# One product of 512 columns in four output projections

## The chip, the core and the metric

The kernel runs on one core of a Trainium2 chip. The metric is the device time of one launch in microseconds (us). Lower is better. All weights stay in HBM and are streamed in once per launch; the residual stream `x` (256 tokens, 2048 features) stays in SBUF from the first to the last layer.

## What is computed

Two model blocks run one after the other on one sequence of 256 tokens. All that matters here is where the output projections stand in them; everything is in float32.

```python
def first_block(x, ...):
    for l in range(2):
        h = rms_norm(x, norm_g[l])
        ...                                   # three kinds of attention on h
        x = x + y @ w_out[l]                  # 2048 x 2048: a changed projection
    return rms_norm(x, final_g)

def second_block(x, ...):
    for layer in range(2):
        x = layer_norm(ALPHA * x + mixers[layer](x), *ln1[layer])      # not changed
        x = layer_norm(ALPHA * x + conv_ffn(x, *ffns[layer]), *ln2[layer])

def conv_ffn(x, w_gate, w_val, conv_w, conv_b, w_down):
    h = causal_dwconv(x @ w_gate, conv_w) + conv_b
    return (jax.nn.silu(h) * (x @ w_val)) @ w_down      # 5632 x 2048: a changed projection
```

## The kernel before

Activations lie feature by token: a tile is 128 features (partitions) by 256 tokens (columns), so `x` is 16 tiles. A weight matrix is cut into output tiles of 128 features, and each of these into blocks of 128 by 128, one for each 128 input features. 1024 columns of such blocks (8 blocks, 512 KB) are one load, numbered `n` in the order of the whole program; the last load of a `down` tile has 4 blocks.

To keep float32 precision with the one-pass type fp32r, each operand is held in two parts: a high part (the value rounded to fp32r) and a low part (the rest). A block's product is three matmuls of 256 columns that add up in one PSUM region: high weight by high `x`, high weight by low `x`, low weight by high `x` (`col`, lines 1948 to 1950). Each matmul loads its own 128 x 128 weights, so the high weight block is loaded twice in a row. Such a set of three matmuls is called a block below.

A load passes through four engines. SyncE fetches it to one of `NRAW` = 4 raw buffers (`fetch`, line 3356, waits until the low part of load n - 4 is made). ScalarE makes the high part (`hi`, line 2380; there are `NPAIR` = 4 buffers for pairs, so it waits until TensorE has used load n - 4). VectorE subtracts to make the low part (`lo`, line 2691). TensorE waits for the low part and runs the blocks (`col`), and its last matmul of the load counts `used`.

Every engine runs its own instructions strictly in the order of one plan, written while the kernel is built. `load(n)` (line 482) puts `hi(n + 2)` and `lo(n + 1)` into the plan ahead of the matmuls of load n. `pump()` after each load lets every side generator take one step; among these is `Norm.step` (line 672), which for each pair of `x` tiles centres the tiles (in the layer norms), sums them, squares them on ScalarE (line 2405) and adds the squares, and makes the raw parts for the next stage.

`out_proj` (line 878) is the output projection of four places: `w_out` of both layers of the first block and `down` of both FFNs. Where its argument `first` is given (`w_out`), tiles 0 to 3 run through `four`, which the change leaves alone; tiles 4 to 15 run in the loop at the end. For `down` all 16 tiles run in the loop. The loop takes two output tiles at a time: they share one PSUM bank of 512 columns, 256 each (`col_tile`, line 534), and when both are done VectorE adds the whole bank to two tiles of `x` in one instruction (`x_add`, line 2816, its instruction is profile line 2819), after which the bank is free and the norm's step for the pair is queued. A `w_out` tile has 16 blocks in two loads, a `down` tile 44 blocks in six loads. The mixers of the second block have a projection of their own (`out_half`), which keeps `col_tile`.

Of the kernel before, what the change touches and what calls it, by code (L numbers as in the profile page):

```python
# [320 lines left out]
def v3(ap, n):  # L321
    return ap.rearrange("p (a b) -> p a b", a=n)


def _build(nc, a, out, stages, ctx):
# [172 lines left out]
    side = []  # L498
# [35 lines left out]
    def col_tile(o, keys, rhs, ready, bk, step=8):  # L534
# [10 lines left out]
        return (used, n)  # L545

    def col_group(outs, tiles_, rhs, ready, after, norm=None, done=None):
        for half in range(2):
            for (o, opens), key in zip(outs, tiles_):
                n = load(*key, half)  # L550
                do("col", n, o, rhs, 8 * half, half == 0 and opens, half == 1,
                   [ready_at(ready, 8 * half + q) for q in range(8)], after)
                pump()
                if half and done is not None:
                    done.append((used, n))
            if norm:
                norm.read[half] = (used, n)
        return (used, n)
# [319 lines left out]
    def out_proj(parts, y, ready, alpha, norm, first, xt):  # L878
# [12 lines left out]
        for t in range(4 if first else 0, KT, 2):  # L891
            bk = banks.get()
            p2 = v3(bk.view, 2)
            for j in range(2):
                m = col_tile(p2[:, j, :], parts(t + j), y, ready, bk)
            add(bk, t, m)
        if norm.free is None:
# [1037 lines left out]
    def tensor_program(e):  # L1935
# [4 lines left out]
        def col(n, o, rhs, k0, begin, end, ready, after, part=None):  # L1940
# [10 lines left out]
            if q == c - 1:  # L1951
                last.then_inc(*used(n))

        def row(n, ps, lhs, k0, ready, after):
            (wh, wl), (lh, ll) = pair_of(n), lhs
# [387 lines left out]
        def ret_pv(j, hh):  # L2343
# [6 lines left out]

        steps = dict(norm_cols=norm_cols, col=col, row=row, rms_sq=rms_sq, ln_first=ln_first, norm_sums=norm_sums, scores=scores,
                     p_turn=p_turn, pv=pv, rope_mm=rope_mm, ukv_k=ukv_k, ukv_v=ukv_v, uq=uq, head_sum=head_sum,
# [329 lines left out]
    def vector_program(e):  # L2682
# [133 lines left out]
        def x_add(sid, bk, t, alpha, m, xt):  # L2816
# [3 lines left out]
                                   op1=ADD).then_inc(*vec("x_add", sid, t))  # L2820

        def q_scale(j):
            w.on([j.q_m])
# [444 lines left out]
        def ret_decay(j, hh):  # L3268
# [5 lines left out]
            else:  # L3274
# [5 lines left out]
                     norm_acc=norm_acc, norm_var=norm_var, norm_R=norm_R, norm_ln=norm_ln, norm_rms=norm_rms, norm_cols=norm_cols, gains=gains, raw_lo=raw_lo,  # L3280
                     lead_fix=lead_fix, lead_scale=lead_scale, x_add=x_add,
                     q_scale=q_scale, k_scale=k_scale, k_copy=k_copy, gate_evict=gate_evict, rope_mm=rope_mm, rope_fin=rope_fin,
# [266 lines left out]
```

## Time and profile before

| what | value |
|---|---|
| time, median of 3 runs | 3592.99 us (3585.59 to 3611.3) |
| span of the profiled execution, first to last instruction | 3590.3 us |
| TensorE matmul busy | 95% of the span, 30164 matmuls |
| VectorE busy | 64% |
| ScalarE busy | 45% |
| mean granted TensorE clock | 0.975 |
| HBM read | 581.31 MB, 162 GB/s over the span |

The profile is of one execution. Its page shares out the span by engine and by line; views of the trace show single instructions with their start and duration. The duration shown for a matmul is the time through the array (some 280 ns for one of 256 columns) and overlaps that of the next, so a matmul's price is read from the distance between two starts, or from the number of matmuls in a stretch. The weight loads have rows of their own (engine PEld).

### The profile page before, as it was taken

The numbers are of one execution on the slowest core, as the hardware profiler recorded it, in microseconds if no ns is written. First come the engines' busy times: TensorE is split into PE (matmuls) and PEld (weight loads), VectorE is DVE, ScalarE is ACT, GpSimd is POOL, SyncE is SP. The second block draws the span as 40 slices with busy tenths as digits, with TensorE's granted clock in tenths as the row PEclk, the third lists the DMA queues.
The fourth block names the chain that finished last, engine by engine and source line by source line (L and its number), as shares of the span: only waits on it lengthen the run. The fifth ranks groups of instructions, "written<-read, shape, count | busy, mean of one in ns | idle before, by whom it ended". The sixth has DMA issues, their size and how long they took to land.

```text
span 3590.3 us, 68886 instructions
## 1 busy us (share of the span) xinstructions
PE 3425.7 (95%) x30164; PEld 3358.8 (94%) x30164; DVE 2281.9 (64%) x3711; ACT 1603.8 (45%) x2267; POOL 81.6 (2%) x101
## 2 busy tenths in 40 slices
PE   7899999999998998999999999988998999999997
PEld 7899999999998888899999999987998999999997
DVE  5656556556676678697666655687545976666555
ACT  4544445444445523255444444562433554444443
POOL 0000000000000001000000000002000000000000
PEclk9999999999999989999999999999999999999998
DMA  6455555555454322255555666541443556656664
GB/s 227 146 176 172 169 176 177 174 179 171 159 194 134 106 66 69 82 171 182 194 189 197 196 191 192 188 131 64 166 158 112 169 174 198 195 189 197 193 195 132
DMA packets 162637, 587.88 MB, mean 164 GB/s; under 512 B 18144, under 2 KB 18144, under 8 KB 161952
## 3 DMA queue, kind: packets, MB, share of 16 engines
q1 hardware_dynamic: 160848, 575.06, 49.0%
q0 software_dynamic: 1488, 8.42, 0.7%
q8 instruction: 236, 3.87, 0.4%
q14 instruction: 65, 0.53, 0.1%
HBM read 581.31 MB, written 2.10 MB: 162 GB/s over the span
## 4 chain that ended last, share of the span: by engine, by line
PE 51%; DVE 9%; ACT 1%; issue 1%; POOL 0%; ACTq 0%; DVEq 0%; POOLq 0%
PE bank L1948 15%; PE bank L1950 15%; PE bank L1949 15%; DVE pairs L2691 2%; DVE xs L2807 1%; DVE xs L2805 1%; PE bank L2127 0%; PE bank L1963 0%; PE bank L1964 0%; PE bank L1965 0%; DVE xr L2695 0%; PE bank L2114 0%; DVE xr L2775 0%; DVE right L3133 0%; PE bank L2104 0%
## 5 line engine op out<-in xcount | busy, mean ns | idle before, releaser
L1948 PE MATMUL bank<-xr,pairs 128*128 128x256 f32 (+1 forms) x5920 | 1675.2, 283 | 62.1 <-DVE pairs L2691 50.7
L1949 PE MATMUL bank<-xr,pairs 128*128 128x256 f32 (+1 forms) x5920 | 1650.9, 279 | 0.0
L1950 PE MATMUL bank<-xr,pairs 128*128 128x256 f32 (+1 forms) x5920 | 1650.5, 279 | 0.0
L2380 ACT ACTIVATE pairs<-raw 128x1024 fp32r<-128x1024 f32 x1108 | 1144.4, 1043 | 980.7 <-PE bank L1950 867.0
L2691 DVE TENSOR_TENSOR pairs<-raw,pairs 128x1024 fp32r<-128x1024 f32 x1108 | 1312.8, 1203 | 324.3 <-ACT pairs L2380 321.9
L1948 PEld LDWEIGHTS bank<-xr,pairs 128*128 128x128 f32 x5920 | 1124.0, 190 | 75.9 <-DVE pairs L2691 58.8
L1949 PEld LDWEIGHTS bank<-xr,pairs 128*128 128x128 f32 x5920 | 1123.0, 190 | 1.6
L1950 PEld LDWEIGHTS bank<-xr,pairs 128*128 128x128 f32 x5920 | 1123.5, 190 | 0.0
L1948 PE MATMUL bank<-parts,pairs 128*128 128x256 f32 x1792 | 497.4, 278 | 3.6 <-DVE parts L2695 3.3
L1949 PE MATMUL bank<-parts,pairs 128*128 128x256 f32 x1792 | 495.6, 277 | 0.0
L1950 PE MATMUL bank<-parts,pairs 128*128 128x256 f32 x1792 | 495.6, 277 | 0.0
L1948 PEld LDWEIGHTS bank<-parts,pairs 128*128 128x128 f32 x1792 | 337.3, 188 | 4.5 <-DVE pairs L2691 3.8
L1949 PEld LDWEIGHTS bank<-parts,pairs 128*128 128x128 f32 x1792 | 337.2, 188 | 0.2
L1950 PEld LDWEIGHTS bank<-parts,pairs 128*128 128x128 f32 x1792 | 337.2, 188 | 0.0
L3107 DVE TENSOR_SCALAR arena<-bank,vec 128x256 f32<-128x256 f32 x88 | 47.8, 543 | 229.9 <-PE bank L1950 229.9
L2819 DVE SCALAR_TENSOR_TENSOR xs<-xs,bank 128x512 f32<-128x512 f32 x64 | 43.7, 686 | 174.6 <-PE bank L1950 174.5
L1963 PE MATMUL bank<-pairs,xr 128*128 128x256 f32 x512 | 149.1, 291 | 0.0
L1965 PE MATMUL bank<-pairs,xr 128*128 128x256 f32 x512 | 143.4, 280 | 0.0
L1964 PE MATMUL bank<-pairs,xr 128*128 128x256 f32 x512 | 143.3, 280 | 0.0
L1963 PEld LDWEIGHTS bank<-pairs,xr 128*128 128x128 f32 x512 | 97.0, 189 | 0.8
L1964 PEld LDWEIGHTS bank<-pairs,xr 128*128 128x128 f32 x512 | 96.9, 189 | 0.7
L1965 PEld LDWEIGHTS bank<-pairs,xr 128*128 128x128 f32 x512 | 96.7, 189 | 0.0
(589 smaller groups left out, 3122.4 us busy)
## 6 DMA issues: line engine op xcount, KB each, us to landing
raw<-in_w_in SPq DMA_DIRECT2D x176, 512.0 KB, 4.3
raw<-in_gate SPq DMA_DIRECT2D x176, 512.0 KB, 4.7
raw<-in_val SPq DMA_DIRECT2D x176, 512.0 KB, 4.0
raw<-in_down SPq DMA_DIRECT2D x160, 512.0 KB, 4.5
raw<-in_l_w_in SPq DMA_DIRECT2D x146, 512.0 KB, 3.9
raw<-in_w_out SPq DMA_DIRECT2D x64, 512.0 KB, 4.6
raw<-in_l_w_out SPq DMA_DIRECT2D x64, 512.0 KB, 3.7
raw<-in_v_in SPq DMA_DIRECT2D x48, 512.0 KB, 4.7
```

Source lines behind the costliest of these rows:

```text
L1948: mm(o, wh[:, q, :], rh[:, k, :], start=begin and q == 0, stop=False)
L1949: mm(o, wh[:, q, :], rl[:, k, :], start=False, stop=False)
L1950: last = mm(o, wl[:, q, :], rh[:, k, :], start=False, stop=end and q == c - 1)
L1963: mm(o, lh[:, k, ms], wh[:, q, :], start=k == 0 and m == 0, stop=False)
L1964: mm(o, ll[:, k, ms], wh[:, q, :], start=False, stop=False)
L1965: last = mm(o, lh[:, k, ms], wl[:, q, :], start=False, stop=k == KT - 1)
L2380: e.activation(pair_of(n)[0], v3(raw_of(n), widths[n] // slices[n]), ACT.Copy).then_inc(*hi_made(n))
L2691: e.tensor_tensor(lo_, v3(raw_of(n), widths[n] // slices[n]), hi_.bitcast(F32), SUB).then_inc(*lo_made(n))
L2805: e.tensor_tensor(xp, xp, two(N.a2), MUL).then_inc(*vec("scaled", N.id, t))
L2807: e.tensor_tensor(xp, xp, two(N.a1), ADD).then_inc(*vec("minus", N.id, t))
L2819: e.scalar_tensor_tensor(out=x[:, t:t + 2, :], in0=x[:, t:t + 2, :], scalar=alpha, in1=v3(bk.view, 2), op0=MUL, op1=ADD).then_inc(*vec("x_ ...
L3107: e.tensor_scalar(b, p2[:, 0, :], VC(f"cw2_{l}", t), VC(f"cb_{l}", t), MUL, ADD).then_inc(*vec("conv2", j.id))
```

## The change

In the loop of `out_proj` each output tile gets a PSUM bank of its own. The high weight block is loaded once and meets a moving operand of 512 columns, made of the high part and the low part of `x` as two runs of 256: the left half of the bank collects high by high, the right half high by low. The low weight block then meets the high part of `x` as before and adds to the left half. VectorE adds both halves to `x` in two instructions per tile, the second waiting for the first. The rest (order of loads, the pumps, the norm's step after each second tile) keeps its place. `parts(t + j)` and the loads are the same.

```diff
+    def wide_tile(bk, keys, rhs, ready):
+
+        k = 0
+        for key in keys:
+            n = load(*key)
+            c = widths[n] // 128
+            do("wide", n, bk, rhs, k, key is keys[0], key is keys[-1], [ready_at(ready, k + q) for q in range(c)])
+            pump()
+            k += c
+        return (used, n)
...
         for t in range(4 if first else 0, KT, 2):
-            bk = banks.get()
-            p2 = v3(bk.view, 2)
             for j in range(2):
-                m = col_tile(p2[:, j, :], parts(t + j), y, ready, bk)
-            add(bk, t, m)
+                bk = banks.get()
+                m = wide_tile(bk, parts(t + j), y, ready)
+                do("x_add_wide", sid, bk, t + j, alpha, m, xt[t] if xt else [])
+                banks.put(bk, (vec, "x_add", sid, t + j))
+            side.append(norm.step(t, (vec, "x_add", sid, t + 1)))
...
+        def wide(n, bk, rhs, k0, begin, end, ready):
+            (wh, wl), (rh, rl), c = pair_of(n), rhs, widths[n] // 128
+            o = v3(bk.view, 2)
+            w.wait_ge(*lo_made[n])
+            if begin:
+                w.on(bk.after)
+            for q in range(c):
+                k = k0 + q
+                w.on(ready[q])
+                a, b = rh[:, k, :], rl[:, k, :]
+                hl = bass.AP(a.tensor, a.offset, [a.ap[0], (b.offset - a.offset, 2), a.ap[-1]])
+                mm(o, wh[:, q, :], hl, start=begin and q == 0, stop=False)
+                last = mm(o[:, 0, :], wl[:, q, :], a, start=False, stop=end and q == c - 1)
+            last.then_inc(*used(n))
...
+        def x_add_wide(sid, bk, t, alpha, m, xt):
+            p2 = v3(bk.view, 2)
+            w.on([m])
+            w.on(xt)
+            e.scalar_tensor_tensor(out=x[:, t, :], in0=x[:, t, :], scalar=alpha, in1=p2[:, 0, :], op0=MUL,
+                                   op1=ADD).then_inc(*vec("x_add_hi", sid, t))
+            w.wait_ge(*vec["x_add_hi", sid, t])
+            e.tensor_tensor(x[:, t, :], x[:, t, :], p2[:, 1, :], ADD).then_inc(*vec("x_add", sid, t))
```

## Rows read from the trace of the kernel before

**Rows 1.** The page: span, then busy us (share) and instructions of each engine.

```profile
span 3590.3 us, 68886 instructions
...
PE 3425.7 (95%) x30164; PEld 3358.8 (94%) x30164; DVE 2281.9 (64%) x3711; ACT 1603.8 (45%) x2267; POOL 81.6 (2%) x101
```

**Rows 2.** The page: the chain that ended last, share of span by line.

```profile
PE bank L1948 15%; PE bank L1950 15%; PE bank L1949 15%; DVE pairs L2691 2%; DVE xs L2807 1%; DVE xs L2805 1%; PE bank L2127 0%; PE bank L1963 0%; PE bank L1964 0%; PE bank L1965 0%; DVE xr L2695 0%; PE bank L2114 0%; DVE xr L2775 0%; DVE right L3133 0%; PE bank L2104 0%
```

**Rows 3.** Four changed stretches: length; busy PE, PEld, DVE, ACT, POOL; clock; DMA share; GB/s.

```profile
482.30:538.80 56.50, 56.50 (x482) 56.50 (x482) 29.91 (x36) 22.77 (x24) 0.00 (x0) 1.00 0.57 187
974.60:1029.00 54.40, 54.40 (x482) 54.40 (x482) 33.92 (x45) 26.24 (x34) 0.00 (x0) 1.00 0.62 200
2126.20:2305.80 179.60, 179.60 (x1587) 179.60 (x1586) 101.27 (x120) 77.52 (x89) 0.00 (x0) 1.00 0.63 194
3386.10:3565.60 179.50, 179.50 (x1585) 179.36 (x1583) 95.28 (x107) 71.28 (x75) 0.00 (x0) 1.00 0.58 179
```

**Rows 4.** Timeline of VectorE, adds of two tiles each: start us, duration us.

```profile
493.51 0.69 DVE L2819 SCALAR_TENSOR_TENSOR xs<-xs,bank 128x512 f32<-128x512 f32 x1 [5.28 <-PE bank L1950]
504.82 0.69 DVE L2819 SCALAR_TENSOR_TENSOR xs<-xs,bank 128x512 f32<-128x512 f32 x1 [5.28 <-PE bank L1950]
...
985.49 0.69 DVE L2819 SCALAR_TENSOR_TENSOR xs<-xs,bank 128x512 f32<-128x512 f32 x1 [4.06 <-PE bank L1950]
...
996.37 0.69 DVE L2819 SCALAR_TENSOR_TENSOR xs<-xs,bank 128x512 f32<-128x512 f32 x1 [4.06 <-PE bank L1950]
...
2186.26 0.69 DVE L2819 SCALAR_TENSOR_TENSOR xs<-xs,bank 128x512 f32<-128x512 f32 x1 [4.42 <-PE bank L1950]
2216.18 0.69 DVE L2819 SCALAR_TENSOR_TENSOR xs<-xs,bank 128x512 f32<-128x512 f32 x1 [4.42 <-PE bank L1950]
```

**Rows 5.** Timeline of TensorE and its weight loads inside a `down` tile.

```profile
2200.00 0.28 PE L1948 MATMUL bank<-parts,pairs 128*128 128x256 f32 x1
2200.01 0.19 PEld L1949 LDWEIGHTS bank<-parts,pairs 128*128 128x128 f32 x1
2200.12 0.28 PE L1949 MATMUL bank<-parts,pairs 128*128 128x256 f32 x1
2200.12 0.19 PEld L1950 LDWEIGHTS bank<-parts,pairs 128*128 128x128 f32 x1
```

**Rows 6.** Timeline of TensorE: plain float32 matmuls with 256 and with 2 columns.

```profile
110.76 1.89 PE L2009 MATMUL bank<-arena 128*128 128x256 f32 x8
...
1505.96 3.63 PE L2092 MATMUL bank<-con,arena 128*128 128x2 f32 x32
```

**Rows 7.** Groups of VectorE instructions by shape: count, busy us, mean ns, idle before.

```profile
L2691 DVE TENSOR_TENSOR pairs<-raw,pairs 128x1024 fp32r<-128x1024 f32 x1068 | 1286.7, 1222 | 306.1 <-ACT pairs L2380 303.7
...
L2819 DVE SCALAR_TENSOR_TENSOR xs<-xs,bank 128x512 f32<-128x512 f32 x64 | 43.7, 686 | 174.6 <-PE bank L1950 174.5
...
L3117 DVE TENSOR_TENSOR arena<-arena,bank 128x256 f32<-128x256 f32 x88 | 36.4, 413 | 0.0
...
L2826 DVE SCALAR_TENSOR_TENSOR arena<-bank,arena 128x256 f32<-128x256 f32 x32 | 13.6, 424 | 98.3 <-PE bank L1950 98.3
...
L3249 DVE SCALAR_TENSOR_TENSOR hs<-hs,vec,bank 128x256 f32<-128x256 f32 x8 | 3.8, 475 | 2.9 <-PE bank L2104 2.9
```

**Rows 8.** Timeline of VectorE just after the add at 2216.18.

```profile
2216.79 2.35 DVE L2691 TENSOR_TENSOR pairs<-raw,pairs 128x1024 fp32r<-128x1024 f32 x2
...
2219.78 0.42 DVE L2726 TENSOR_TENSOR nbuf<-nbuf,xs 128x256 f32<-128x256 f32 x1
2220.24 0.42 DVE L2728 TENSOR_TENSOR nbuf<-nbuf,xs 128x256 f32<-128x256 f32 x1
```

**Rows 9.** The chain that ended last, where the last projection ends.

```profile
3565.54 0.13 PE bank L1950
3565.69 0.70 DVE xs L2819
```

**Rows 10.** DMA issues of `down` weights: count, KB each, median us from issue to landing.

```profile
raw<-in_down SPq DMA_DIRECT2D x160, 512.0 KB, 4.5
```

More of the change, by code:

```diff
@@ L2349, in ret_pv @@
             mm(ps[:, 128:T], s["v"][:, 1, hh, :], s["A"][:, T:T + 128], start=False, stop=True).then_inc(*pe("ret_pv", j.pr, hh))
-        steps = dict(norm_cols=norm_cols, col=col, row=row, rms_sq=rms_sq, ln_first=ln_first, norm_sums=norm_sums, scores=scores,
+        steps = dict(norm_cols=norm_cols, col=col, wide=wide, row=row, rms_sq=rms_sq, ln_first=ln_first, norm_sums=norm_sums, scores=scores,
                      p_turn=p_turn, pv=pv, rope_mm=rope_mm, ukv_k=ukv_k, ukv_v=ukv_v, uq=uq, head_sum=head_sum,
@@ L3280, in vector_program @@
                      norm_acc=norm_acc, norm_var=norm_var, norm_R=norm_R, norm_ln=norm_ln, norm_rms=norm_rms, norm_cols=norm_cols, gains=gains, raw_lo=raw_lo,
-                     lead_fix=lead_fix, lead_scale=lead_scale, x_add=x_add,
+                     lead_fix=lead_fix, lead_scale=lead_scale, x_add=x_add, x_add_wide=x_add_wide,
                      q_scale=q_scale, k_scale=k_scale, k_copy=k_copy, gate_evict=gate_evict, rope_mm=rope_mm, rope_fin=rope_fin,
```

## The prediction

> **What bounds the kernel now.** I read the page's shares first: TensorE is busy for 95% of a span of 3590.3 us, VectorE for 64%, ScalarE for 45% [rows 1]. The chain that ended last says the same by line: 45% of the span is the three matmuls of `col`, and the next line, VectorE's low parts, has 2% [rows 2]. Shares of the whole say little about one stage, so I read the stretches of the four changed projections. In each of them TensorE is busy all the time at a granted clock of 1.00 (its 2.4 GHz level), with VectorE at 53 to 62% and the DMA engines at 57 to 63% [rows 3]. So in these stages time is the number of blocks times the price of a block, and nothing else.
>
> That price comes from the distance between two adds, since each add waits for the end of a pair of tiles. In `down` a pair has 2 x 44 = 88 blocks and takes 2216.18 - 2186.26 = 29.92 us, which is 340.0 ns a block or 113.3 ns a matmul. In `w_out` of layer 1 a pair has 32 blocks and takes 10.88 us: 340.0 ns too. In `w_out` of layer 0 it takes 11.31 us: 353.3 ns a block, 117.8 ns a matmul [rows 4]. The same instructions at the same clock have two paces here. 1585 to 1587 matmuls in 179.5 us confirm the first (113.2 ns), 482 in 56.5 us the second (117.2 ns) [rows 3].
>
> **What sets 113.3 ns.** 256 columns at 2.4 GHz are 106.7 ns, so a matmul costs 6.6 ns more than its columns. Inside a `down` tile every weight load starts within 0.01 us after a matmul has started, and the next matmul starts 0.11 us later [rows 5]. The matmuls with only 2 columns show what is left when there is almost nothing to stream: 32 of them take 3.63 us; less the last one's own 0.25 us that is some 109 ns from start to start [rows 6]. So loading weights takes about 109 ns, and matmuls of 256 columns are paced by it, just above their columns. The opposite case is the plain float32 matmul of line 2009: 8 records take 1.89 us; less the last one's 0.38 us that is 1.51 / 7 = 215.7 ns each [rows 6]. This is 512 / 2.4 = 213.3 plus 2.4 ns; I take it for 512 steps of the array, during which the weight load is hidden and only a small fixed cost remains.
>
> **The change, part by part.** (1) The wide matmul. It replaces two matmuls and one weight load. The nearest row is line 2009's 215.7 ns against 2 x 113.3 = 226.7 ns now. From below it is bounded by its columns, 213.3 ns; from above I use the slower pace of `w_out`, 2 x 117.8 = 235.6 ns. I take 215.7, because it is the row in which the array has the same 512 steps and a weight load runs beneath it.
>
> (2) The low weight's matmul keeps its 256 columns and, beneath it, the load of the next high weight, so it keeps its 113.3 ns (bounds: 109 and 117.8). A block is then 215.7 + 113.3 = 329.0 ns instead of 340.0: 11.0 ns less. Over the two `down` projections this is 2 x 16 x 44 = 1408 blocks x 11.0 = 15.5 us. Over `w_out` of layer 1, 12 x 16 = 192 blocks, 2.1 us. In `w_out` of layer 0 I let the narrow matmul keep its slow pace: 353.3 - 215.7 - 117.8 = 19.8 ns x 192 = 3.8 us. If the slow pace ended there, it would be 24.3 x 192 = 4.7 us. Sum: -21.4 us.
>
> The Trainium skill gives the same two prices, and I cite it as it also holds a rule that would give another result: "TensorE: Matmul & The Clock Gate", section "Back-to-back issue gap", has N / 2.4 + 2.5 ns for warm matmuls, 216 ns for 512 columns, where line 2009 shows 215.7. For the streams of load and matmul of real kernels the same section gives about 131 ns at 512 columns. By that figure the four stages would lose some 171 us; this is the rival "far more" below.
>
> (3) VectorE's adds. A pair had one of 686 ns. A tile now has two of 256 columns. The first is like line 2826's (424 ns) or, if the scalar costs what it does with a vector operand, line 3249's (475 ns); the second like line 3117's, 413 ns [rows 7]. Dependent instructions of this size start 0.46 us apart at 0.42 us each [rows 8], so a tile's add takes 0.46 + 0.41 = 0.87 us (0.92 with 475 ns), 1.74 us a pair, 1.05 us more than now. For 28 pairs (6 + 6 + 8 + 8) that is 29 us more work on VectorE. It is covered where TensorE never waits for it: in a `down` pair VectorE is busy 56% of 29.9 us, so 13 us are idle and 1.05 is asked for [rows 3, 4].
>
> (4) The order on VectorE. Now it stands at an add once per tile, not once per pair, until TensorE has ended the tile. Queued behind it is the low part two loads ahead of the one just ended; the next load's is made already. After the end at T the add starts 0.04 us later (the last matmul's slot ends at 3565.54 + 0.11, the add starts at 3565.69 [rows 9]), takes 0.87 us, and the low part 1.15 to 1.22 us (2.35 for two [rows 8], mean 1222 ns [rows 7]): ready at T + 2.13. TensorE needs it when it has run the load between, 8 x 0.329 = 2.63 us. So 0.5 us of cover is left (it is 0.8 us now), and I cost this at nothing. If the cover went, each 0.1 us over it would cost 56 tiles x 0.1 = 5.6 us. What is late next behind a late low part is SyncE's fetch of the load four on: it leaves at T + 2.1, lands 4.5 us later [rows 10], and its high and low part take some 2.3 us more, T + 8.9 in all; TensorE comes to it five loads after T, at 13.2 us.
>
> In `w_out` a tile lasts only 16 x 0.329 = 5.26 us. The stretch of layer 1 is the tightest: 33.9 us of VectorE in 5 pairs [rows 3], 6.8 a pair, with the wide adds 7.8 of 10.5 us. It still fits.
>
> (5) Ends. At the end of each projection the last add lies open on the chain: now 0.70 us for the pair [rows 9], after the change 0.87 for the last tile (the other tile's is done before). 4 x 0.17 = +0.7 us.
>
> (6) PSUM banks, 14 or 16 taken in turn instead of half as many: 8 exist, a bank comes back after eight tiles when its add is long done. The count of loads, bytes and pumps does not change. Both are costed at zero.
>
> **Sum.** -15.5 - 2.1 - 3.8 + 0.7 = -20.7 us. Made against the profiled execution this is 3590.3 - 20.7 = 3569.6 us of span. The median of the runs shown lies 2.7 us above that span, so I predict 3593.0 - 20.7 = 3572.3 us, 0.6% less.
>
> **The rivals.**
>
> *The cost sticks to each instruction.* The 6.6 ns over the columns belong to every matmul with its load, whatever its length. Then the wide matmul is 213.3 + 6.6 = 220 ns, a block 333.3, and the gain 6.7 x 1600 + (353.3 - 220 - 117.8 = 15.5) x 192 - 0.7 = 13 us: 3580 us. For it: no fp32r matmul in the trace is longer than its weight load. Against it: line 2009. Chance 0.15.
>
> *The two streams disturb each other (the other side).* The two paces of [rows 4] show that something beyond count and clock slows matmuls by 4.5 ns in this kernel. The wide matmul reads two runs of `x` far apart, with the low weight's load beneath the first; now each of the three matmuls meets its weight load in a pattern that lasts for the whole stage. If all blocks went to 353.3 ns, 1600 x 13.3 + 0.7 = 22 us are lost: 3615 us. It decides from a wide matmul above 226.7 ns. Against it: the weight load has twice the time beneath a wide matmul. To be over 1% slower the wide matmul would have to cost 226.7 + 36 / 1792 x 1000 = 247 ns. Chance 0.12, 0.05 of it beyond that. The Trainium skill speaks against this rival: by the same page, section "Step-by-step: what each phase is for", streaming and weight loading have read ports of their own, so that loading takes nothing from the running matmul; by that rule alone the sum above stands, but it doesn't account for the two paces in [rows 4].
>
> *VectorE becomes late.* The gain is used up when each tile loses 20.7 / 56 = 0.37 us, that is when add and low part take 0.87 us more than I count; 1% slower needs 1.0 us a tile. Chance 0.05, 0.03 of it beyond 1%: 3593 to 3630 us.
>
> *It does not do what it says.* The wide product is cut into two of 256 columns with a weight load each, and only the adds differ: 3594 us. Chance 0.04.
>
> *Far more.* The columns alone are 768 / 2.4 = 320 ns a block, 20 x 1600 + 33.3 x 192 = 38 us: 3555 us. By the price of 131 ns (above) it would be 3422 us. Against both: 256 columns take 113.3 ns, more than one step of the clock each. Chance 0.04.
>
> **How the numbers follow.** The forecast has 0.60, the rivals 0.15, 0.12, 0.05, 0.04 and 0.04. The forecast's own range is 3565 to 3582 us. The range of 8 in 10 reaches down to the columns' bound (3556) and up past the case of no gain with the spread of the three runs, to 3602; it leaves out the rest of the disturbed case and of the late VectorE. About 1% (36 us) is what a measurement of this kernel can tell from no change. Faster by more than that is only the last rival, 0.04; slower by more is 0.05 + 0.03 = 0.08; within 1% is 0.88.
>
> **What would show it.** After the change the page should have 1792 matmuls and as many weight loads fewer (28372). In the wide line's stretches a wide matmul should be followed 0.216 us later by the narrow one and that 0.113 us later by the next wide one; two adds of `down` tiles should stand 44 x 0.329 = 14.48 us apart. A distance of 14.67 would be the first rival, 15.5 the second. TensorE's waits for low parts in these stretches should stay at none; any shows the third. The forecast is wrong if the wide matmul takes over 227 ns, or if TensorE is idle after a tile's end.

## The result

The changed kernel takes 3614.98 us (median of 20 runs, 3602.16 to 3644.37), the kernel before 3603.70 us (median of 20 runs taken with them, 3585.59 to 3629.54). The ratio is 1.0046, with a 95% interval of 1.0027 to 1.0066. So the change costs about 3603.7 x 0.0046 = 16.6 us (9.7 to 23.8); the two medians alone lie 11.3 us apart, inside that interval. The forecast was a gain of 20.7 us; the time went the other way, and 3614.98 lies above the range's upper end of 3602. The three runs shown of before gave 3593.0 us, 10.7 us less than the median of twenty. What follows therefore goes by ratios and by stages, not by the old median.

The page of the changed kernel, with the lines that answer to [rows 1, 2]: its span, the busy time of each engine, and the chain that ended last.

```profile
span 3629.1 us, 65412 instructions
...
PE 3465.9 (96%) x28372; PEld 3317.0 (91%) x28372; DVE 2304.2 (63%) x3795; ACT 1605.3 (44%) x2267; POOL 81.9 (2%) x101
...
PE bank L1960 11%; PE bank L1961 11%; PE bank L1962 11%; PE bank L1977 9%; PE bank L1978 5%; DVE pairs L2718 2%; DVE xs L2834 0%; PE bank L2154 0%; DVE xs L2832 0%; PE bank L1990 0%; PE bank L1992 0%; PE bank L1991 0%; DVE right L3169 0%; PE bank L2141 0%; DVE xr L2722 0%
```

The matmuls are 28372, 1792 fewer, and the chain is TensorE's as before. Lines 1960 to 1962 are `col`'s three matmuls, 1977 the wide one, 1978 the narrow one. Fewer matmuls keep TensorE busy for 40 us longer. The adds of the changed kernel say where, on VectorE's timeline (start, duration; in brackets how long VectorE had been idle, and for whom):

```profile
984.56 0.42 DVE L2853 SCALAR_TENSOR_TENSOR xs<-xs,bank 128x256 f32<-128x256 f32 x1 [0.92 <-PE bank L1978]
...
990.21 0.42 DVE L2853 SCALAR_TENSOR_TENSOR xs<-xs,bank 128x256 f32<-128x256 f32 x1 [2.50 <-PE bank L1978]
...
2178.92 0.42 DVE L2853 SCALAR_TENSOR_TENSOR xs<-xs,bank 128x256 f32<-128x256 f32 x1 [4.69 <-PE bank L1978]
2179.38 0.42 DVE L2856 TENSOR_TENSOR xs<-xs,bank 128x256 f32<-128x256 f32 x1
2179.72 1.22 DVE L2718 TENSOR_TENSOR pairs<-raw,pairs 128x1024 fp32r<-128x1024 f32 x1
...
2194.47 0.42 DVE L2853 SCALAR_TENSOR_TENSOR xs<-xs,bank 128x256 f32<-128x256 f32 x1 [4.68 <-PE bank L1978]
```

A `down` tile takes 2194.47 - 2178.92 = 15.55 us, which is 353.4 ns for each of its 44 blocks; a `w_out` tile of layer 1 takes 5.65 us, 353.1 ns for each of 16. The prediction wanted 14.48 us for `down`. 340.0 ns, the price of before, would be 14.96 [rows 4]. All four stages now stand at the slower of the two paces that [rows 4] shows. `w_out` of layer 0 stood there already in the profile of before.

The next timeline is TensorE's, where the last gate and value projection ends and `down` of layer 1 begins:

```profile
3354.69 0.28 PE L1962 MATMUL bank<-xr,pairs 128*128 128x256 f32 x1
3354.80 0.39 PE L1977 MATMUL bank<-parts,pairs 128*128 128x512 f32 x1
3355.03 0.28 PE L1978 MATMUL bank<-parts,pairs 128*128 128x256 f32 x1
3355.15 0.40 PE L1977 MATMUL bank<-parts,pairs 128*128 128x512 f32 x1
3355.38 0.28 PE L1978 MATMUL bank<-parts,pairs 128*128 128x256 f32 x1
```

Up to 3354.80 a matmul starts 0.11 us after the one before it. From there on a wide one starts every 0.353 us: the narrow one follows it after 0.235 us, and the next wide one 0.118 us after that. The very first wide one is an exception: the narrow one follows it after 0.226 us, and its record is 0.39 us long where the later ones have 0.40. So the wide matmul costs twice a narrow one, first at the fast pace (2 x 113.3) and then at the slow one (2 x 117.8). It is never near 0.216.

**Where the profiled spans differ.** Against before's stages, `down` has 16 pairs x (31.10 - 29.92) = +18.9 us, `w_out` of layer 1 has 6 x (11.30 - 10.88) = +2.5, the four ends about +0.7: 22.1 us. But the spans differ by 3629.1 - 3590.3 = 38.8. The rest lies in a stage that the change doesn't touch, the gate and value projections of layer 0's feed-forward. Busy time by stretch of 100 us (columns as in [rows 3]), first the kernel before, then the changed one:

```profile
1740.00:1840.00 100.00, 100.00 (x885) 100.00 (x884) 64.08 (x85) 46.64 (x57) 0.00 (x0) 1.00 0.59 192
```

```profile
1740.00:1840.00 100.00, 100.00 (x852) 100.00 (x851) 60.79 (x80) 45.34 (x53) 0.00 (x0) 1.00 0.57 185
```

885 matmuls are 113.0 ns each, 852 are 117.4 ns, both with a granted clock of 1.00. Over the stage's 1408 blocks, at 353.3 - 340.0 = 13.3 ns each, that is 18.7 us (all other stages together took 2.0 us less). The instructions of this stage are the same. The experiments show that the difference is one of two executions and not of two kernels: e1 has wide matmuls in the same places and 885 matmuls in this stretch, and e3 has none and 851.

### The profile page after: what moved, and what is told of

The parts are those of the page before. It is cut to its first block, busy times and chain, and to the rows that moved or that the text cites. A ratio compares the mean times of both kernels' runs of the same rounds, so it can differ in the third digit from the quotient of the medians.

```text
span 3629.1 us, 65412 instructions
## 1 busy us (share of the span) xinstructions
PE 3465.9 (96%) x28372; PEld 3317.0 (91%) x28372; DVE 2304.2 (63%) x3795; ACT 1605.3 (44%) x2267; POOL 81.9 (2%) x101
## 4 chain that ended last, share of the span: by engine, by line
PE 52%; DVE 9%; ACT 1%; issue 1%; POOL 0%; ACTq 0%; DVEq 0%; POOLq 0%
PE bank L1960 11%; PE bank L1961 11%; PE bank L1962 11%; PE bank L1977 9%; PE bank L1978 5%; DVE pairs L2718 2%; DVE xs L2834 0%; PE bank L2154 0%; DVE xs L2832 0%; PE bank L1990 0%; PE bank L1992 0%; PE bank L1991 0%; DVE right L3169 0%; PE bank L2141 0%; DVE xr L2722 0%
## 5 line engine op out<-in xcount | busy, mean ns | idle before, releaser
L1960 PE MATMUL bank<-xr,pairs 128*128 128x256 f32 (+1 forms) x5728 | 1631.6, 285 | 61.7 <-DVE pairs L2718 50.9
L1961 PE MATMUL bank<-xr,pairs 128*128 128x256 f32 (+1 forms) x5728 | 1607.5, 281 | 0.0
L1962 PE MATMUL bank<-xr,pairs 128*128 128x256 f32 (+1 forms) x5728 | 1607.3, 281 | 0.0
L1960 PEld LDWEIGHTS bank<-xr,pairs 128*128 128x128 f32 x5728 | 1097.5, 192 | 74.6 <-DVE pairs L2718 58.4
L1961 PEld LDWEIGHTS bank<-xr,pairs 128*128 128x128 f32 x5728 | 1090.5, 190 | 1.7
L1962 PEld LDWEIGHTS bank<-xr,pairs 128*128 128x128 f32 x5728 | 1089.9, 190 | 0.0
L1977 PE MATMUL bank<-parts,pairs 128*128 128x512 f32 x1600 | 565.9, 398 | 0.0
L1978 PE MATMUL bank<-parts,pairs 128*128 128x256 f32 x1600 | 449.6, 281 | 0.0
L1977 PEld LDWEIGHTS bank<-parts,pairs 128*128 128x128 f32 x1600 | 300.8, 188 | 74.1
L1978 PEld LDWEIGHTS bank<-parts,pairs 128*128 128x128 f32 x1600 | 300.4, 188 | 0.1
L2853 DVE SCALAR_TENSOR_TENSOR xs<-xs,bank 128x256 f32<-128x256 f32 x56 | 23.6, 421 | 197.0 <-PE bank L1978 197.0
L2432 ACT ACTIVATE nbuf<-xs 128x512 f32<-128x512 f32 x56 | 35.5, 634 | 136.7 <-DVE xs L2748 88.3
L1960 PE MATMUL bank<-yr,pairs 128*128 128x256 f32 x256 | 77.4, 302 | 10.9 <-DVE yr L2722 9.4
```

The source lines that it names most:

```text
L1960: mm(o, wh[:, q, :], rh[:, k, :], start=begin and q == 0, stop=False)
L1961: mm(o, wh[:, q, :], rl[:, k, :], start=False, stop=False)
L1962: last = mm(o, wl[:, q, :], rh[:, k, :], start=False, stop=end and q == c - 1)
L1977: mm(o, wh[:, q, :], hl, start=begin and q == 0, stop=False)
L1978: last = mm(o[:, 0, :], wl[:, q, :], a, start=False, stop=end and q == c - 1)
L2432: e.activation(N.sq, x[:, t:t + 2, :], ACT.Square).then_inc(*act("norm_sq", N.id, t))
```

## The experiments

Each edit is against the changed kernel unless it says otherwise.

**e1_swap.** Which run meets which weight load. The low part's run comes first, and the low weight's matmul adds into the right half.

```diff
-hl = bass.AP(a.tensor, a.offset, [a.ap[0], (b.offset - a.offset, 2), a.ap[-1]])
+hl = bass.AP(a.tensor, b.offset, [a.ap[0], (a.offset - b.offset, 2), a.ap[-1]])
-last = mm(o[:, 0, :], wl[:, q, :], a, ...)
+last = mm(o[:, 1, :], wl[:, q, :], a, ...)
```

> The wide matmul streams the low part of x first, then the high part; the low weight adds to the right half. Nothing else differs from the change. Theory P (pairing: pace depends on which 512-byte half of memory the weight load reads beneath the run that streams; in the old order load and run always stood 192 bytes apart, in the change the low weight's load lies beneath the high run, half a kilobyte off): here the low weight's load lies beneath the low run again, so the wide matmul should go from 235.3 ns to about 226.7 ns or less and a block from 353.3 to 340 ns or less, the ratio to before 0.995 to 1.000. Theory L (length: a matmul that streams 512 columns of this type without a break runs at the slow pace of 117.7 ns per 256, whatever is loaded beneath it): still 235.3 and 353.3, ratio about 1.005.

Measured: 3617.49 us against 3609.22, ratio 1.0039 (0.9998 to 1.0079). Its TensorE in a `down` tile:

```profile
2180.04 0.40 PE L1977 MATMUL bank<-parts,pairs 128*128 128x512 f32 x1
2180.28 0.28 PE L1978 MATMUL bank<-parts,pairs 128*128 128x256 f32 x1
2180.39 0.40 PE L1977 MATMUL bank<-parts,pairs 128*128 128x512 f32 x1
```

Still 0.235 and 0.118. It doesn't matter under which run the low weight is loaded.

**e2_split.** The wide product alone is undone; banks and adds per tile stay.

```diff
-mm(o, wh[:, q, :], hl, start=begin and q == 0, stop=False)
+mm(o[:, 0, :], wh[:, q, :], a, start=begin and q == 0, stop=False)
+mm(o[:, 1, :], wh[:, q, :], b, start=False, stop=False)
```

> The change with the wide matmul undone alone: three matmuls of 256 columns with three weight loads, but a bank per tile and two adds per tile as in the change. If the loss comes from the wide matmul's pace (both theories), blocks are back at 340.0 ns in the down stages (or at 353.3 in whole stages that happen to run at the slow pace, as before), no wait of TensorE for a low part appears, and the ratio to before is 1.000 (at most +0.7 us for the ends). If the adds or the banks cost anything, the distance of two adds in a down tile is over 14.96 us and the ratio stays near 1.005.

Measured: 3607.11 us, ratio 0.9994 (0.9956 to 1.0033). Its adds in `down`, and in `w_out` of layer 0:

```profile
2168.62 0.42 DVE L2853 SCALAR_TENSOR_TENSOR xs<-xs,bank 128x256 f32<-128x256 f32 x1 [4.42 <-PE bank L1978]
...
2183.58 0.42 DVE L2853 SCALAR_TENSOR_TENSOR xs<-xs,bank 128x256 f32<-128x256 f32 x1 [4.42 <-PE bank L1978]
...
489.99 0.42 DVE L2853 SCALAR_TENSOR_TENSOR xs<-xs,bank 128x256 f32<-128x256 f32 x1 [1.71 <-PE bank L1978]
...
495.64 0.42 DVE L2853 SCALAR_TENSOR_TENSOR xs<-xs,bank 128x256 f32<-128x256 f32 x1 [2.51 <-PE bank L1978]
```

`down` is back at 14.96 us a tile, 340.0 ns a block. The loss in `down` is the wide matmul's alone; banks and adds cost nothing that can be seen there. Both `w_out` stages take 5.65 us a tile here, the slow pace, with no wide matmul in the kernel.

**e3_pair_order.** The kernel before, with `col`'s first two products exchanged, so that the other run of `x` meets the low weight's load.

```diff
-mm(o, wh[:, q, :], rh[:, k, :], start=begin and q == 0, stop=False)
-mm(o, wh[:, q, :], rl[:, k, :], start=False, stop=False)
+mm(o, wh[:, q, :], rl[:, k, :], start=begin and q == 0, stop=False)
+mm(o, wh[:, q, :], rh[:, k, :], start=False, stop=False)
```

> The kernel before, with the first two matmuls of every block of col in the other order (high weight by low x, then by high x). Counts and columns stay; only which weight load lies beneath which run changes: two of three pairs are now half a kilobyte off. Theory P: two of three matmuls, or all of them, slow from 113.3 to 117.7 ns in all stages of col, a block takes 349 to 353 ns also in the gate and down stages, the time grows by some 40 to 80 us. Theory L: no change, 340.0 ns where a stage is fast, time within 20 us of before.

Measured: one run of 3609.08 us. Adds of pairs, in `w_out` of layer 1 and in `down`:

```profile
978.27 0.69 DVE L2819 SCALAR_TENSOR_TENSOR xs<-xs,bank 128x512 f32<-128x512 f32 x1 [2.20 <-PE bank L1950]
989.57 0.69 DVE L2819 SCALAR_TENSOR_TENSOR xs<-xs,bank 128x512 f32<-128x512 f32 x1 [4.49 <-PE bank L1950]
...
2173.59 0.69 DVE L2819 SCALAR_TENSOR_TENSOR xs<-xs,bank 128x512 f32<-128x512 f32 x1 [4.42 <-PE bank L1950]
2203.51 0.69 DVE L2819 SCALAR_TENSOR_TENSOR xs<-xs,bank 128x512 f32<-128x512 f32 x1 [4.42 <-PE bank L1950]
```

`down` keeps 29.92 us a pair, and `w_out` of layer 1 has moved to 11.30. Layer 0's gate and value stage stands at 851 matmuls per 100 us. By this one run alone the exchange could have done that; e9 shows that an unchanged kernel's stages change pace too. For `down` it is clear: the pairing doesn't set the pace, and a slow gate and value stage ahead of `down` doesn't make `down` slow either.

**e4_same_run.** The 512 columns are the high part twice. The low part of `x` is left out of the product.

```diff
-hl = bass.AP(a.tensor, a.offset, [a.ap[0], (b.offset - a.offset, 2), a.ap[-1]])
+hl = bass.AP(a.tensor, a.offset, [a.ap[0], (0, 2), a.ap[-1]])
```

> The change, but the 512 columns are the high part of x twice (the product with the low part is left out). It tells a jump between two far runs (theory J) from length: under J the wide matmul has no second place to go to, 226.7 ns or less; under P the high run stands over the low weight's load all the time, 235 ns or more; under L 235.3 ns. The narrow one stays at 113.3 or 117.7.

Measured: one run of 3642.28 us. Two adds in `down` lie 2186.50 - 2170.95 = 15.55 us apart, and on TensorE's timeline a wide matmul is followed after 0.235 us by the narrow one, that one after 0.118. The distance between two runs of `x` isn't the cause. The long time of this one run isn't explained by the edit alone: the gate and value stage, which it doesn't touch, ran 852 matmuls per 100 us here as well.

**e5_mix.** Wide matmuls only in every second pair of tiles; the other tiles have three narrow ones.

```diff
+if stream[n][-2] // 2 % 2:
     mm(o, wh[:, q, :], hl, ...)
     last = mm(o[:, 0, :], wl[:, q, :], a, ...)
+else:
+    mm(o[:, 0, :], wh[:, q, :], a, ...)
+    mm(o[:, 1, :], wh[:, q, :], b, ...)
+    last = mm(o[:, 0, :], wl[:, q, :], a, ...)
```

> The change, but every other pair of tiles (2 and 3, 6 and 7, 10 and 11, 14 and 15) keeps the wide matmul and the rest have three narrow ones, all with a bank and two adds per tile. Theory L (a matmul of 512 columns has a price of its own, 235.3 ns, and narrow ones keep theirs): down tiles alternate between 44 x 340 = 14.96 us and 44 x 353.3 = 15.55 us. Theory S (state: the pace of 113.3 or 117.7 ns is a state of the stream that only a break or another kind of work changes, and one wide matmul tips it to the slow side): from the first wide tile on the narrow tiles too take 15.55 us, up to the next break. If wide matmuls were only slow by the chance of the stage, some wide tiles would take 14.96.

Measured: one run of 3604.08 us. The adds of the first tiles of `down`; the releaser is line 1983 after a narrow tile and 1979 after a wide one:

```profile
2075.69 0.42 DVE L2858 SCALAR_TENSOR_TENSOR xs<-xs,bank 128x256 f32<-128x256 f32 x1 [4.42 <-PE bank L1983]
...
2090.65 0.42 DVE L2858 SCALAR_TENSOR_TENSOR xs<-xs,bank 128x256 f32<-128x256 f32 x1 [4.42 <-PE bank L1983]
...
2107.05 0.42 DVE L2858 SCALAR_TENSOR_TENSOR xs<-xs,bank 128x256 f32<-128x256 f32 x1 [4.69 <-PE bank L1979]
...
2122.60 0.42 DVE L2858 SCALAR_TENSOR_TENSOR xs<-xs,bank 128x256 f32<-128x256 f32 x1 [4.69 <-PE bank L1979]
...
2138.15 0.42 DVE L2858 SCALAR_TENSOR_TENSOR xs<-xs,bank 128x256 f32<-128x256 f32 x1 [4.69 <-PE bank L1983]
```

The second narrow tile takes 14.96 us. From the first wide tile on every tile takes 15.55, the narrow ones too (the one that ends ahead of 2138.15, and all behind it), in both layers. The first wide tile's 16.40 us also hold other work that TensorE does there once; in e2, without wide matmuls, the same tile takes 15.85. This is the clearest row of the study: wide matmuls aren't dearer than the slow pace, they bring it on, and narrow ones behind them stay in it here (e7 has a tile where they don't).

**e6_lengths.** In `down`, all but the first block of a tile are two matmuls of one length over a contiguous run, for six lengths, in pairs of tiles; the products are thus others.

```diff
+run = bass.AP(s.tensor, s.offset, [s.ap[0], (1, size)])
+mm(bk.view[:, 0:size], wh[:, q, :], run, start=False, stop=False)
+last = mm(bk.view[:, 0:size], wl[:, q, :], run, start=False, stop=end and q == c - 1)
```

> Down tiles with blocks of two matmuls of one length each, high and low weight by the same contiguous run: tiles 2 and 3 of 256 columns, then 272, 320, 384, 448 and 512 in tiles 12 and 13; tiles 0 and 1 narrow, 14 and 15 as in the change. Products are replaced, so the output is not the reference's; only prices are read. My prediction's rule (load-paced up to some length, then columns / 2.4 + 2.4 ns): 113.3, 115.7, 135.7, 162.4, 189.1, 215.7 ns. Theory R (the stream of this type has a rate below one column a clock: 0.4427 ns a column where fast, 0.4596 where slow): fast 113.3, 120.4, 141.7, 170, 198.3, 226.7; slow 117.7, 125.0, 147.1, 176.5, 205.9, 235.3. I expect slow from 272 on.

Measured: one run of 3581.96 us, with less work in `down`, so that its time says nothing. As distances of adds, the tile between the first two adds shown has 320 columns, the next 384, that between 2208.13 and 2225.88 has 448, the last one 512:

```profile
2146.95 0.42 DVE L2865 SCALAR_TENSOR_TENSOR xs<-xs,bank 128x256 f32<-128x256 f32 x1 [2.70 <-PE bank L1983]
...
2159.91 0.42 DVE L2865 SCALAR_TENSOR_TENSOR xs<-xs,bank 128x256 f32<-128x256 f32 x1 [3.21 <-PE bank L1983]
...
2175.15 0.42 DVE L2865 SCALAR_TENSOR_TENSOR xs<-xs,bank 128x256 f32<-128x256 f32 x1 [4.55 <-PE bank L1983]
...
2208.13 0.42 DVE L2865 SCALAR_TENSOR_TENSOR xs<-xs,bank 128x256 f32<-128x256 f32 x1 [5.71 <-PE bank L1983]
2225.88 0.42 DVE L2865 SCALAR_TENSOR_TENSOR xs<-xs,bank 128x256 f32<-128x256 f32 x1 [5.43 <-PE bank L1983]
2246.30 0.42 DVE L2865 SCALAR_TENSOR_TENSOR xs<-xs,bank 128x256 f32<-128x256 f32 x1 [6.96 <-PE bank L1983]
```

A tile is one block of 0.35 us and 86 matmuls. 12.96 us give 146.6 ns for 320 columns, 15.24 give 173.1 for 384, 17.75 give 202.3 for 448, 20.42 give 233.4 for 512. That is 0.451 to 0.458 ns a column for each of them (between the two paces' 0.443 and 0.460), 1.08 to 1.10 steps of 2.4 GHz, where the prediction's rule (a column a step and 2.4 ns) gives 135.7, 162.4, 189.1 and 215.7. The extra cost goes with the columns. It isn't a fixed piece that a longer matmul spreads out. TensorE waited between loads in the tiles of 256 and 272 columns, so that their adds say nothing on this. Inside a load their matmuls do: two of 256 columns start 0.113 us apart, and 15 distances of 272 columns in a row (2125.14 to 2126.99) are 0.123 us each, 0.453 ns a column, where the rule gives 0.116.

This run's `w_out` of layer 0 also holds a change of pace. The edit leaves its tiles 4 to 13 with three narrow matmuls and gives tiles 14 and 15 wide ones:

```profile
521.28 0.42 DVE L2865 SCALAR_TENSOR_TENSOR xs<-xs,bank 128x256 f32<-128x256 f32 x1 [1.49 <-PE bank L1990]
526.72 0.42 DVE L2865 SCALAR_TENSOR_TENSOR xs<-xs,bank 128x256 f32<-128x256 f32 x1 [2.29 <-PE bank L1990]
532.36 0.42 DVE L2865 SCALAR_TENSOR_TENSOR xs<-xs,bank 128x256 f32<-128x256 f32 x1 [1.70 <-PE bank L1986]
```

Tile 13, like the eight before it, takes 5.44 us, and tile 14, the first wide one, 5.64: as in e5, the slow pace comes with the wide matmuls. In layer 1 the narrow `w_out` tiles of this run take 5.65 us from the start, with no wide one ahead of them in the stage.

**e7_types.** In `down`, pairs of tiles with bf16 operands, with contiguous fp32r runs, with another order, and with narrow ones; all but each tile's first block are replaced, so again the products are others.

```diff
+if g in (1, 2):
+    h16, l16 = (z.bitcast(B16)[:, 1:256:2] for z in (wh[:, q, :], wl[:, q, :]))
+    m16 = con[:, 0:256].bitcast(B16) if g == 1 else run.bitcast(B16)[:, 1:1024:2]
+    mm(bk.view, h16, m16, start=False, stop=False)
+    last = mm(o[:, 0, :], l16, m16[:, 0:256], start=False, stop=end and q == c - 1)
```

> Down tiles of the change with other kinds of wide matmul (products replaced or reordered, the output is not the reference's): tiles 2 and 3: bf16, 512 contiguous columns, then bf16 256; 4 and 5: bf16 with every second element (the same bytes as fp32r); 6 and 7: fp32r, one contiguous run of 512 of x; 8 and 9: fp32r, a contiguous run from the weight buffer; 10 and 11: as the change but the narrow matmul first; 12 and 13: three narrow ones, the low weight's second; the rest as the change. Theory R (rate of the fp32r stream): bf16 at 215.7 and 109 to 113 ns, all fp32r runs of 512 at 235.3, wherever they lie and whatever the order. If the rate comes from the bytes read per column and not from the type, the bf16 with every second element is at 235 too. If a far second run were the cause, the contiguous ones are at 226.7 or 215.7. Theory S adds: the narrow tiles 12 and 13 stay at 117.7.

Measured: one run of 3600.69 us. Below stand TensorE with packed bf16 (read from the constants, `con`); with bf16 values 4 bytes apart, read from `x`'s parts; and the adds around the two tiles in which three narrow fp32r matmuls a block follow one wide block:

```profile
2111.98 0.38 PE L1986 MATMUL bank<-con,pairs 128*128 128x512 bf16 x1
2112.20 0.27 PE L1987 MATMUL bank<-con,pairs 128*128 128x256 bf16 x1
2112.31 0.38 PE L1986 MATMUL bank<-con,pairs 128*128 128x512 bf16 x1
...
2139.73 0.39 PE L1986 MATMUL bank<-parts,pairs 128*128 128x512 bf16 x1
2139.96 0.27 PE L1987 MATMUL bank<-parts,pairs 128*128 128x256 bf16 x1
2140.07 0.39 PE L1986 MATMUL bank<-parts,pairs 128*128 128x512 bf16 x1
```

```profile
2246.47 0.42 DVE L2875 SCALAR_TENSOR_TENSOR xs<-xs,bank 128x256 f32<-128x256 f32 x1 [4.41 <-PE bank L1993]
...
2261.44 0.42 DVE L2875 SCALAR_TENSOR_TENSOR xs<-xs,bank 128x256 f32<-128x256 f32 x1 [4.42 <-PE bank L1997]
...
2276.98 0.42 DVE L2875 SCALAR_TENSOR_TENSOR xs<-xs,bank 128x256 f32<-128x256 f32 x1 [4.69 <-PE bank L1997]
```

Packed bf16 takes 0.216 us for 512 columns and 0.109 for 256: the price that I had expected of fp32r. bf16 values 4 bytes apart take 0.226 and 0.114. fp32r takes 0.235 and 0.118 from a contiguous run of `x` and also with the narrow matmul first (15.53 to 15.55 us a tile), and on average 0.2325 and 0.117 from a weight buffer (15.40). So there are two steps. From 216 to 226 ns the type need not change: the bf16 weights are the same in both pairs of tiles, and only the streamed operand differs, by its step of 4 bytes and by its buffer, which this run doesn't tell apart. 226 and 114 are just the prices of fp32r at its fast pace (2 x 113.3 = 226.7), whose values also lie 4 bytes apart. Only the step from 226 to 235, the slow pace, was seen under fp32r alone. The last three adds hold a limit of what I know: the two tiles have the same instructions and one wide block at their start, and the tile ahead of them ran at the slow pace, yet the first takes 14.97 us and the second 15.54, in layer 1 as in layer 0. A wide matmul doesn't bring the slow pace on every time, and narrow ones don't always keep it.

**e8_bf16_cross.** The kernel before, with the two cross products of `down` in bf16, whose weight loads and matmuls should both be cheaper.

```diff
+h16, l16 = (z.bitcast(B16)[:, 1:256:2] for z in (wh[:, q, :], wl[:, q, :]))
+mm(o, h16, rl[:, k, 0:T], start=False, stop=False)
+last = mm(o, l16, rl[:, k, T:2 * T], start=False, stop=end and q == c - 1)
```

> The kernel before (pairs of tiles, one add a pair), but in the two down projections the two cross products run in bf16: high weight (its upper 16 bits, read in place) by a bf16 low part of x, and low weight (upper 16 bits) by a bf16 copy of x, both of these packed where the fp32r low part lay, at the price of one more ScalarE copy per u tile. Matmuls, weight loads and columns stay as before; two of three moving operands have 2 bytes a column instead of 4. Theory R (the price of a column of fp32r is the stream's own, packed bf16 is not taxed): a block is 113.3 + 109 + 109 = 331 ns where fast and about 336 where the fp32r one is slow, down tiles take 14.6 to 14.8 us (a pair 29.2 to 29.6), the time falls by 8 to 25 us, ratio 0.993 to 0.998. My prediction's rule (paced by the weight loads, whatever streams): 340.0 ns, a pair 29.92 us, ratio 1.000.

Measured: 3614.95 us against 3596.75, ratio 1.0041 (1.0015 to 1.0067); a pair takes 31.21 us, 354.7 ns a block. TensorE and its loads:

```profile
2200.45 0.36 PE L1955 MATMUL bank<-parts,pairs 128*128 128x256 f32 x1
2200.66 0.10 PEld L1958 LDWEIGHTS bank<-low,pairs 128*128 128x128 bf16 x1
2200.66 0.28 PE L1958 MATMUL bank<-low,pairs 128*128 128x256 bf16 x1
```

The bf16 load starts 0.21 us after the fp32r matmul, together with its own matmul; among matmuls of one type a load starts within 0.01 us of the matmul that it runs beneath [rows 5]. By its parts a block is 113.3 + 2 x 109 = 331.3 ns and it costs 354.7. The 23 ns over that I put down to changing the type there and back, which e10 tests.

**e9_before_again.** The kernel before, unchanged.

> The kernel before, unchanged, profiled once more. Theory S (the two paces are states that a stage falls into when it starts, by chance from run to run): the stages needn't have the paces of the first profile; w_out of layer 0 may run at 340.0 and a gate stage at 353.3. If the pace were fixed by code and addresses, all stages repeat the first profile: w_out of layer 0 at 353.3, of layer 1 and both down stages at 340.0.

Measured: one run of 3582.68 us. Adds in `w_out` of layer 0:

```profile
494.43 0.69 DVE L2819 SCALAR_TENSOR_TENSOR xs<-xs,bank 128x512 f32<-128x512 f32 x1 [4.86 <-PE bank L1950]
505.31 0.69 DVE L2819 SCALAR_TENSOR_TENSOR xs<-xs,bank 128x512 f32<-128x512 f32 x1 [4.86 <-PE bank L1950]
```

`w_out` of layer 0 takes 10.88 us a pair, where the same kernel took 11.31 in [rows 4]. In that stage the pace belongs to the execution and not to the kernel. The gate and value stage of layer 0 shows the same: of the twelve profiles, nine have it at 113 ns and three at 118 (the changed kernel's, e3's and e4's). A step of 18.7 us for that stage is thus in the spread of every kernel's times. The narrow `down` stages took 340.0 ns a block in every profile that has them (before, e2, e3, e9).

**e10_bf16_grouped.** e8's types, grouped: for each load of weights the 8 fp32r products first, then the 16 bf16 ones.

```diff
+for q in range(c):
+    mm(o, wh[:, q, :], rh[:, k0 + q, :], ...)
+for q in range(c):
+    mm(o, h16, rl[:, k0 + q, 0:T], start=False, stop=False)
+    last = mm(o, l16, rl[:, k0 + q, T:2 * T], start=False, ...)
```

> As the run with bf16 cross products in the down projections, but within each load of 8 blocks the 8 fp32r products come first and the 16 bf16 ones after them, so the type changes twice per load instead of twice per block. There a block took 354.7 ns where its three matmuls alone promise 113.3 + 2 x 109 = 331.3. Theory T (each change of type costs: some 23 ns per block were lost to it, and packed bf16 is indeed untaxed): a load takes 8 x 331.3 + 23 = 2.67 us against 2.72 in the kernel before, a pair of down tiles 29.4 us instead of 29.9, the ratio is 0.996 to 0.999. If instead the bf16 matmuls themselves are slow here (their operands lie in another buffer, their weights are read with a step), the pair stays near 31.2 us and the ratio near 1.004.

Measured: 3590.92 us against 3595.37, ratio 0.9983 (0.9959 to 1.0007). Adds of two pairs:

```profile
2157.73 0.69 DVE L2839 SCALAR_TENSOR_TENSOR xs<-xs,bank 128x512 f32<-128x512 f32 x1 [4.36 <-PE bank L1959]
2187.32 0.69 DVE L2839 SCALAR_TENSOR_TENSOR xs<-xs,bank 128x512 f32<-128x512 f32 x1 [4.36 <-PE bank L1959]
```

29.59 us a pair instead of 29.92: 0.33 x 16 = 5.3 us in `down`. 11 loads of 8 x 113.3 + 16 x 109 = 2650 ns are 29.15 us; the other 0.44 us are 40 ns a load for two changes of type. Inside a group the bf16 matmuls do start 0.109 us apart, from the same buffers as in e8, so it is the changes that cost and not the bf16 matmuls. The gain is in the trace and agrees in size with the 4.5 us between the medians, but the interval holds no change. Of the versions timed more than once it has the lowest ratio, and its time isn't settled to be less.

## Why the prediction was wrong

**The step that failed is (1), through the paragraph on what sets 113.3 ns.** I read the 6.6 ns over the columns as the weight load's pace, which a longer matmul would hide, and took line 2009's 215.7 ns as the nearest row. The 32 two-column records and line 2009 [rows 6] are plain float32, the projections are fp32r. What the runs showed in their place: an fp32r matmul of 512 columns costs 235.3 ns, and 226 in the first record of `down`, which is twice the narrow one's 113.3. Lengths of 272 to 512 columns cost 0.451 to 0.458 ns a column in e6. Packed bf16 of 512 columns does take 216 ns (e7), and 226 with its values 4 bytes apart. So of the 19.6 ns by which (1) was short some 11 are the price of such columns at the fast pace, and some 9 the slow pace. A block is 768 columns of fp32r whether in two matmuls or three, 340 or 353.3 ns. The saved weight load was worth nothing. Removing instructions from a stream whose price goes by columns was the error, and my upper bound of 235.6 ns for (1), from the slow pace of `w_out`, was the value that came.

The profile of before had a row that I passed over. At a granted clock of 0.50 (the 1.2 GHz level; columns of the first row as in [rows 3]) the same fp32r matmuls start 0.213 us apart:

```profile
442.00:447.00 5.00, 4.86 (x23) 4.89 (x24) 3.47 (x8) 2.41 (x6) 0.00 (x0) 0.50 0.42 121
```

```profile
442.92 0.41 PE L1948 MATMUL bank<-xr,pairs 128*128 128x256 f32 x1
...
443.77 0.41 PE L1949 MATMUL bank<-xr,pairs 128*128 128x256 f32 x1
```

Four distances take 0.85 us, 213 ns each, and 256 columns at 1.2 GHz are 213.3: nothing is left over. So the surplus at 2.4 GHz is neither a fixed 6.6 ns for each matmul nor a fixed number of the array's steps. It looks like a limit of some 0.44 ns a column beside the array's own (an estimate, 113.3 / 256), which only shows when the array could go faster. No run says what sets it.

The rule of the Trainium skill that I had weighed, "TensorE: Matmul & The Clock Gate", section "Back-to-back issue gap" (N / 2.4 + 2.5 ns), agrees with the packed bf16 runs of e7 (0.216 and 0.109 us); for fp32r the traces differ from it, 235.3 ns for 512 columns, and the measurement decides. It didn't give both of my prices, as I wrote: by it 256 columns are 109.2 ns, where the profile of before has 113.3.

**Step (2)** took 113.3 ns for the narrow matmul and got 118, its upper bound, since all four stages ran at the slow pace. I had let the slow pace of `w_out` in layer 0 stand as a thing of that stage. The rows of before held two paces for one instruction; I should have asked what moves a stage from one to the other before I priced a new instruction at the better one.

**The rival "two streams disturb each other"** gave the number: 353.3 ns a block in all four stages, 22 us, 3615 us. Its mechanism fell. Neither the run that meets the low weight's load (e1, e3) nor the two runs of `x` (e4, and the contiguous run of e7) changes the price. So the number of this rival was right and its reason was not. What holds of it is that the pattern lasts: wide fp32r matmuls bring on the slow pace, and narrow ones behind them keep it in e5. The Trainium skill's rule that I set against this rival, own read ports for streaming and loading (same page, "Step-by-step: what each phase is for"), isn't contradicted: pairing loads and runs otherwise did nothing in e1. The rival "the cost sticks to each instruction" (220 ns) fell with e6, where the surplus grows with the columns. "Far more" fell too: no matmul of 512 columns took less than 0.215 us in any run. (Its 171 us take every block from the fast pace; by the same steps as the forecast it would be 84.7 x 1792 = 152 and 21, less 0.7, some 172.)

**Steps (3), (5) and (6) came as worked out, and (4) in its outcome.** Of VectorE's adds the first starts 0.46 us before the second, each takes 0.42: 0.88 us a tile. TensorE waits for no low part in any of the four stages. One reading in (4) was off: in the profile of before the last matmul starts at 3565.38, so that its slot ends at 3565.49 and the add follows after 0.20 us, not 0.04. In the `down` tile of the changed kernel that ends ahead of 2178.92, the last matmul's slot ends at 2178.72, the low part is ready at 2179.72 + 1.22 = 2180.94, and TensorE needs it at 2178.72 + 8 x 0.353 = 2181.54: 0.6 us of cover. At the forecast's pace it would have been 0.4 instead of 0.5. e2 keeps these adds and banks and takes 0.9994 of before. At the very end the two adds begin 0.2 us after the last matmul's slot and are over 0.87 us later. The count of 28372 came exactly.

**The sum.** 22.1 us by the stages of the two profiles, of which 2.5 hold only when before's `w_out` of layer 1 is at the fast pace. Since the two `w_out` stages of before are sometimes slow already, and the changed kernel's have nothing more to lose there, its typical loss by these prices should lie between the 18.9 + 0.7 = 19.6 us of `down` with the ends and, with both `w_out` stages fast before, 24.6. The measured 16.6 us lie below this, but the interval reaches to 23.8; the unchanged stage's steps of 18.7 us are the noise in it.

**What stays open.** Nothing here shows what the two paces are in the chip, why narrow `down` stages never left the fast one while `w_out`'s and the gate stage's did, or what decides whether one wide block brings the slow one on (e7). It isn't settled either what makes the fast pace 113.3 instead of 109 ns. That bf16 values 4 bytes apart take 114 and packed ones 109, under the same weights, points to the reading of the streamed columns, but their buffer changed with the step. No run streamed packed bf16 from `x`'s buffer in these tiles, or values 4 bytes apart from `con`.

## What to carry to other kernels

Price a matmul by a row of its own type and layout: line 2009 looked like the same 512 steps and was not the same work. If the price of a stream goes by its columns, as fp32r's does here, merging two matmuls into a longer one saves a record and no time, and can cost the pace of all that stands behind it. And before two profiles are compared, read the pace of every stage from the distance of two equal events, the unchanged stages too: here one untouched stage moved the span by almost as much as the change did.

## What the runs showed of the hardware

- The same fp32r matmul of 256 columns runs at 113.3 or at 117.8 ns, mostly for a whole stage, at a granted clock of 1.00 both times; which one differs between executions of one kernel. At a granted clock of 0.50 it takes 213 ns, its 256 columns and nothing over.
- bf16 matmuls take 216 and 109 ns for 512 and 256 columns with packed values, 226 and 114 with values 4 bytes apart (from another buffer), which is fp32r's fast pace (e7).
- An fp32r matmul of 272 to 512 columns costs 0.451 to 0.460 ns a column (e6 and the changed kernel), where packed bf16 of 512 costs 0.421.
- Changing from fp32r to bf16 and back costs 23 ns in e8 and about 40 in e10; in e8 a bf16 weight load starts 0.21 us after the fp32r matmul ahead of it, not beneath it.
- The record of a bf16 weight load is 0.10 us, of an fp32r one 0.19 us, but the matmuls of 256 columns that run with them take 109 against 113.3 ns.
